# An expert gather of 8 tokens x 16 picks of one head, with the weighted sum in four column positions

## The reference, cut to what matters

```python
def peer_ffn(h, w_query, keys1, keys2, expert_u, expert_v):
    q = (hf @ w_query).reshape(t, PEER_HEADS, 2, PEER_HALF)
    s1 = einsum('thc,hnc->thn', q[:, :, 0], keys1)        # 128 keys a side
    s2 = einsum('thc,hnc->thn', q[:, :, 1], keys2)
    v1, i1 = top_k(s1, 16); v2, i2 = top_k(s2, 16)
    cand_s = v1[..., :, None] + v2[..., None, :]          # 256 candidates
    cand_i = i1[..., :, None] * 128 + i2[..., None, :]
    top_s, top_pos = top_k(cand_s, 16)
    idx = take_along_axis(cand_i, top_pos); gate = softmax(top_s)
    # for every token, 8 heads x 16 picks:
    act = gelu(einsum('thkd,td->thk', expert_u[idx], h))
    out = einsum('thk,thkd->td', gate * act, expert_v[idx])
```

## Time and profile before

| | us |
|---|---|
| median of 3 runs | 3149.2 |
| lowest, highest | 3148.14, 3149.35 |
| span of the profiled execution | 3147.3 |
| begin of the stage `peer` in it | 1745.2 |
| first gather issued | 1761.0 |
| last product of gathered rows begins | 3133.3 |

### The profile page before, as it was taken

One profiled execution on the slowest core, in us unless ns is written; L12 is line 12 of the kernel. 1 busy time (PEld: TensorE's weight loads), 2 busy tenths in 40 slices (PEclk: granted clock), 3 DMA queues, 4 the chain that ended last, 5 costly groups with the idle time before them and its releaser, 6 DMA issues. The chain is left out here.

```text
span 3147.3 us, 27781 instructions
## 1 busy us (share of the span) xinstructions
PE 2714.7 (86%) x10052; PEld 1434.7 (46%) x10052; DVE 1357.1 (43%) x3261; ACT 590.2 (19%) x1357; POOL 708.3 (23%) x622
## 2 busy tenths in 40 slices
PE   8999697877888888769989899999988888888887
PEld 5755343333333333244768666666543343333332
DVE  2162300000000000044531676667777777777774
ACT  2132100000000000022120222322322322222222
POOL 0000000000000000001420233334434444444442
PEclk9899799999888999979999999999999999999989
DMA  4002699999999999531224799999999999999997
GB/s 146 27 21 113 263 426 426 427 426 426 426 424 423 420 418 421 251 137 47 94 67 149 290 426 425 425 418 421 400 426 427 412 426 426 427 414 426 420 421 329
DMA packets 138856, 1049.63 MB, mean 334 GB/s; under 512 B 22032, under 2 KB 23008, under 8 KB 48224
## 3 DMA queue, kind: packets, MB, share of 16 engines
q0 software_dynamic: 82944, 545.32, 41.5%
q1 hardware_dynamic: 55776, 502.53, 38.8%
HBM read 1051.96 MB, written 20.97 MB: 341 GB/s over the span
## 5 line engine op out<-in xcount | busy, mean ns | idle before, releaser
L2184 PE MATMUL psum<-peer_ring,peer_diag 128*128 128x512 f32 x2048 | 956.8, 619 | 154.2 <-ACT peer_diag L2245 154.1
L2037 POOL DMA_INDIRECT peer_ring<-in_peer_uv,peer_pick x512 | 576.5, 1126 | 910.7 <-PE psum L2184 746.6
L2353 DVE CUSTOM_DVE_ANT_0 peer_ring<-peer_ring,sb_rows 128x1024 f32<-128x1024 f32 x512 | 625.1, 1225 | 348.6 <-DMA peer_ring<-in_peer_uv,peer_pick 337.2
L2184 PEld LDWEIGHTS psum<-peer_ring,peer_diag 128*128 128x128 f32 x2048 | 396.6, 198 | 666.3 <-issue 430.7
L1120 PE MATMUL psum<-ffn1w_w,sb_y 128*64 128x512 f32 x1872 | 510.4, 649 | 85.9 <-DMA ffn1w_w<-in_w_up 60.0
L1165 DVE TENSOR_TENSOR sb_y<-psum,sb_y 128x512 f32<-128x512 f32 x32 | 22.1, 692 | 877.0 <-ACT sb_y L1148 877.0
L1120 PEld LDWEIGHTS psum<-ffn1w_w,sb_y 128*64 128x64 f32 x1872 | 176.1, 149 | 346.7 <-issue 345.0
L2245 ACT ACTIVATE peer_diag<-sb_ident,peer_mix 128x128 f32<-128x128 f32 x512 | 178.1, 395 | 683.7 <-DVE peer_mix L2363 681.9
L1141 PE MATMUL psum<-ffn1w_w,moe_hT 128*64 128x512 f32 x864 | 227.8, 598 | 36.0 <-DVE moe_hT L1170 33.7
L1213 POOL DMA_INDIRECT expert_rows<-sb_tiles,ffn_block_tok x32 | 32.3, 1009 | 894.6 <-ACT sb_tiles L1154 894.6
L1516 PE MATMUL psum<-sb_y,sb_tiles 128*128 128x256 f32 (+1 forms) x640 | 189.5, 455 | 17.3 <-ACT mix_Q L1741 8.9
(11 more groups left out here) (429 smaller groups left out, 2498.0 us busy)
## 6 DMA issues: line engine op xcount, KB each, us to landing
ffn1w_w<-in_w_gate SPq DMA_DIRECT2D x64, 2048.0 KB, 31.6
ffn1w_w<-in_w_down SPq DMA_DIRECT2D x54, 2048.0 KB, 35.8
ffn1w_w<-in_w_up SPq DMA_DIRECT2D x53, 2048.0 KB, 34.3
sb_tiles<-in_w_in2b SPq DMA_DIRECT2D x56, 512.0 KB
sb_rows<-in_w_up SPq DMA_DIRECT2D x11, 2048.0 KB, 36.0
sb_rows<-in_w_down SPq DMA_DIRECT2D x10, 2048.0 KB, 32.2
sb_tiles<-in_w_query SPq DMA_DIRECT2D x30, 512.0 KB
sb_tiles<-in_w_out SPq DMA_DIRECT2D x24, 512.0 KB
```

The source lines that it names most:

```text
L2037: pool.indirect_dma_start(out=ring[:, slot], out_offset=None, in_=A["peer_uv"], in_offset=bass.IndirectOffsetOnAxis(ap=pick[:, i, j:j + 1] ...
L2184: last = nc.tensor.matmul(ps[:, BANK[i] + c], diag[:, b % DIAGS, x], ring[:, slot, D + 512 * c:D + 512 * (c + 1)], start=False, stop=end, ...
L2353: dve.tensor_tensor_reduce(ring[:, n % RING, 0:D], ring[:, n % RING, 0:D], hr[:, i], 1.0, 0.0, ALU.mult, ALU.add, dots[:, i, j + x:j + x + ...
```

## The change

Everything but `peer` and its tables stays. What a gather holds, and what follows from it, is changed:

- A gather holds all 16 picks of one head for 8 tokens (row 16a + c is pick c of token a). Four of them, for tokens 8q.. of each 32-token strip, make a batch: (tile, head, quarter q). There are 128 batches of four gathers in place of 256 of two, the ring has 8 slots in place of 10, and a slot is released with its whole batch (`spent` once a batch). The gathers are 512 of 1 MiB as before.
- The weighted sum of a gather takes a 128x32 block, of which 8 columns are nonzero, in place of a 128x128 diagonal: VectorE writes `mix` (128 x 4 x 8) from the turned gates and the gelu, ScalarE's diagonals are gone, and TensorE runs the batch's four gathers into four strips of 32 PSUM partitions: 8 products of 512 columns a batch (`weighted_sum`).
- The dot product needs, in each partition, the row of its own token: `spread` makes it on TensorE (two products with a contraction over 32 rows for each half of 512 columns) and `spread_out` copies it with ScalarE (128x1024, twice a pair) into `hb`, three pairs deep. A pair serves two gathers for as many heads as a set has; the sets are `SETS`: heads 1, 1, 2, 4 in tile 0, 8 in tile 1, 4, 4 in tile 2, 8 in tile 3. That makes 64 pairs, 32 of them in tile 0.
- The picks and gates of a group are turned: VectorE spreads them over 128 columns (`placed`), TensorE multiplies and transposes (`turn`), VectorE and ScalarE copy them out.
- Groups go tile by tile, head by head. The searches keep three pieces and VectorE as their place, but not their even pace: 6 in steps 0 to 28, 8 in steps 30 to 61 (one per 4 steps, a step being two gathers), 8 in steps 102 to 133, 8 in steps 144 to 183 (one per 5).
- Ahead of the first gather TensorE and ScalarE now do three spread pairs, `residual(0)`, `scores(1)` and `turn(0)`. Three more small constants are loaded.
- In the second step of a batch TensorE's weighted sum comes ahead of that step's other products, not behind. The late products stand two steps apart from step 2 to 88; the gates are not stored but go from PSUM through a sigmoid over both halves.

```diff
-RING = 10
+RING = 8
...
+BATCH, QUARTERS = 4, 4
+SETS = ((1, 1, 2, 4), (8,), (4, 4), (8,))
+BATCHES, PER = NT * P * PEER_H * TOPK // P // BATCH, TOPK // BATCH
...
+def _batches():
+    for i, sizes in enumerate(SETS):
+        head = 0
+        for size in sizes:
+            for quarter in range(QUARTERS):
+                QUADS.append((i, quarter, size, len(BATCH_OF)))
+                BATCH_OF.extend((i, hd, quarter) for hd in range(head, head + size))
+            head += size
...
+def last_reader(pair):
+    quad, side = divmod(pair, 2)
+    return BATCH * (QUADS[quad][3] + QUADS[quad][2] - 1) + 2 * side + 1
+
+SPREADS_AT = {}
+for _quad in range(2, len(QUADS)):
+    _start, _wide = QUADS[_quad][3], QUADS[_quad - 1][2] > 1
+    SPREADS_AT.setdefault(_start - (2 if _wide else 1), []).append(2 * _quad)
+    SPREADS_AT.setdefault(_start - 1, []).append(2 * _quad + 1)
+SPREADS_AT.setdefault(0, []).insert(0, 3)
...
+SEARCH = {2: (0, 1, 2), 3: (5, 6, 8), 4: (10, 12, 13), 5: (15, 17, 18), 6: (20, 22, 23), 7: (25, 27, 28)}
+for _g in range(8, 16):
+    _s = 30 + 4 * (_g - 8)
+    SEARCH[_g] = (_s, _s + 1, _s + 3)
+for _g in range(16, 24):
+    _s = 102 + 4 * (_g - 16)
+    SEARCH[_g] = (_s, _s + 1, _s + 3)
+for _g in range(24, 32):
+    _s = 144 + 5 * (_g - 24)
+    SEARCH[_g] = (_s, _s + 2, _s + 4)
...
-    for g in range(10):
-        JOBS_AT.setdefault(8 * g, []).append(("query", 6 + g))
-        if g % 2:
-            JOBS_AT.setdefault(8 * g + 4, []).append(("scores", 3 + g // 2))
-    for j in range(3 * KH + LATE):
-        JOBS_AT.setdefault(4 + 7 * j // 4, []).append(("conv", j) if j < 3 * KH else ("late", j - 3 * KH))
-    JOBS_AT.setdefault(82, []).append(("late_sum", 0))
+    for r, at in zip(range(3, 8), ((0, 1, 3), (5, 6, 8), (10, 11, 13), (15, 16, 18), (20, 21, 23))):
+        for b, job in zip(at, (("query", 2 * r), ("query", 2 * r + 1), ("scores", r))):
+            JOBS_AT.setdefault(b, []).append(job)
+    late = [("conv", j) for j in range(3 * KH)]
+    for m in range(KD):
+        late += [("gate_a", m), ("gate_b", m), ("branch", m)]
+    late += [("result", m) for m in range(KD)]
+    for j, job in enumerate(late):
+        JOBS_AT.setdefault(2 + 2 * j, []).append(job)
+    JOBS_AT.setdefault(2 * len(late) + 5, []).append(("late_sum", 0))
...
+        at = 98 + 4 * h
+        for b, job in ((at, ("query", QUERIES + 2 * h)), (at + 1, ("query", QUERIES + 2 * h + 1)), (at + 3, ("scores", PEER_H + h))):
+            JOBS_AT.setdefault(b, []).append(job)
+    for b, job in ((100, ("rows", 2)), (112, ("rows", 3))):
...
+        near = st.sb("near", [P, 3, 2, P])
+        far = st.sb("far", [P, H, 2, P])
+        work = st.sb("work", [P, 3, HT])
...
+        hb = st.sb("hb", [P, HB, D])
...
-                for n in range(NT * PICKS):
-                    g, slot = n // K, n % RING
-                    i, j = tile_of(g), head_of(g) * K + n % K
-                    if n % K == 0:
+                pool.memset(mix[:], 0.0).then_inc(cleared, 1)
+                for n in range(BATCH * BATCHES):
+                    b, slot = n // BATCH, n % RING
+                    i, hd, quarter = BATCH_OF[b]
+                    g = H * i + hd
+                    if n == BATCH * FIRST_BATCH[g]:
                         pool.wait_ge(picked, g + 1)
                     if n >= RING:
-                        pool.wait_ge(spent, n - RING + 1)
+                        pool.wait_ge(spent, (n - RING) // BATCH + 1)
+                    at = quarter + QUARTERS * (n % BATCH)
                     pool.indirect_dma_start(out=ring[:, slot], out_offset=None, in_=A["peer_uv"],
-                                            in_offset=bass.IndirectOffsetOnAxis(ap=pick[:, i, j:j + 1], axis=0)
+                                            in_offset=bass.IndirectOffsetOnAxis(ap=pick[:, g, at:at + 1], axis=0)
...
+                def spread(pair):
+                    quad, side = divmod(pair, 2)
+                    i, quarter = QUADS[quad][0], QUADS[quad][1]
+                    bank = spread_bank(pair)
+                    pe.wait_ge(r_out, 2 * i + 2)
+                    if pair == 0:
+                        pe.wait_ge(loaded, 80)
+                    if bank == 0:
+                        pe.wait_ge(done, 1)
+                    if bank == 2 and pair > 2 * QUAD_OF[FIRST_BATCH[2 * H]]:
+                        pe.wait_ge(done, 2)
+                    if bank == 0 and pair > 2 * QUAD_OF[FIRST_BATCH[3 * H]]:
+                        pe.wait_ge(done, 3)
+                    for c in range(2):
+                        if pair or c:
+                            pe.wait_ge(hb_out, 2 * pair + c)
+                        for x in range(2):
+                            r = slice(SPAN * (2 * side + x), SPAN * (2 * side + x + 1))
+                            last = nc.tensor.matmul(ps[:, bank + x], copies[r, P * quarter:P * (quarter + 1)],
+                                                    hr[r, i, 512 * c:512 * (c + 1)], start=True, stop=True)
+                        last.then_inc(hb_ps, 1)
+                def turn(g):
+                    pe.wait_ge(placed_in, g + 1)
+                    if g == 0:
+                        pe.wait_ge(loaded, 80)
+                    else:
+                        pe.wait_ge(gates_out, g)
+                    nc.tensor.matmul(ps[:, 5, P:P + K], placed[:, 0], eights[:], start=True, stop=True)
+                    nc.tensor.transpose(ps[:, 5, 0:P], placed[:, 1], ident[:]).then_inc(turned, 1)
...
+                def weighted_sum(b):
+                    i, _, quarter = BATCH_OF[b]
+                    pe.wait_ge(mixed, b + 1)
+                    for c in range(2):
+                        for r in range(BATCH):
+                            slot = (BATCH * b + r) % RING
+                            last = nc.tensor.matmul(ps[SPAN * r:SPAN * (r + 1), sums_bank(i) + c],
+                                                    mix[:, b % DIAGS, r, EDGE - 8 * quarter:EDGE - 8 * quarter + SPAN],
+                                                    ring[:, slot, D + 512 * c:D + 512 * (c + 1)],
+                                                    start=False, stop=b == LAST_BATCH[H * i + H - 1], skip_group_check=True)
+                    last.then_inc(spent, 1)
...
                 scores(0)
                 pe.wait_ge(scaled, 1)
-                rows(0, 0)
-                rows(1, 2)
+                rows(0, 2)
+                pe.wait_ge(s_out, 1)
                 query(2)
                 query(3)
-                pe.wait_ge(r_out, 4)
+                pe.wait_ge(r_out, 2)
+                for pair in range(3):
+                    spread(pair)
                 residual(0)
-                residual(1)
                 scores(1)
+                turn(0)
+                rows(1, 6)
                 query(4)
                 query(5)
                 scores(2)
-                for b in range(BATCHES):
-                    i, j = place(b)
-                    for name, m in JOBS_AT.get(b, ()):
+                turn(1)
+                for step in range(STEPS):
+                    b = step // 2
+                    if step % 2 == 0:
+                        for pair in SPREADS_AT.get(b, ()):
+                            spread(pair)
+                    if step % 2 == 1:
+                        if b in (FIRST_BATCH[H], FIRST_BATCH[2 * H], FIRST_BATCH[3 * H]):
+                            residual(BATCH_OF[b][0])
+                        weighted_sum(b)
...
-                            result(m - OUT)
-                    pe.wait_ge(diagonal, BATCH * (b + 1))
-                    for x in range(BATCH):
-                        slot = (b * BATCH + x) % RING
-                        end = j + x == PICKS - 1
-                        for c in range(2):
-                            last = nc.tensor.matmul(ps[:, BANK[i] + c], diag[:, b % DIAGS, x], ring[:, slot, D + 512 * c:D + 512 * (c + 1)],
-                                                    start=False, stop=end, skip_group_check=True)
-                        last.then_inc(spent, 1)
...
+                    if step - 1 in PICKS_AT:
+                        turn(PICKS_AT[step - 1])
...
+                def spread_out(pair):
+                    bank = spread_bank(pair)
+                    for c in range(2):
+                        act.wait_ge(hb_ps, 2 * pair + c + 1)
+                        if c == 0 and pair >= HB // 2:
+                            act.wait_ge(dotted, last_reader(pair - HB // 2) + 1)
+                        act.activation(hb[:, hb_of(pair):hb_of(pair) + 2, 512 * c:512 * (c + 1)], ps[:, bank:bank + 2],
+                                       ACT.Copy).then_inc(hb_out, 1)
...
-                def diagonals(b):
-                    act.wait_ge(mixed, b + 1)
-                    if b >= DIAGS:
-                        act.wait_ge(spent, BATCH * (b - DIAGS + 1))
-                    for x in range(BATCH):
```

(53 more changed lines are left out.)

338 lines of the change are left out of this document (181 added, 157 removed).

## The result

| | before | after |
|---|---|---|
| median of 4 runs, us | 3149.27 | 3525.04 |
| lowest, highest | 3148.14, 3149.85 | 3519.64, 3532.31 |
| span of the profiled execution | 3147.3 | 3517.8 |

A forecast was written before the change was run, and what follows sets the result against it. The prediction took the kernel before to be bound by DMA bytes. Its terms, mostly late gathers, less 15 for gaps and 2 for the tail, summed to +110 us, giving 3259 us, range 3165 to 3380.

The forecast's parts named there:

- the stream's gaps: Gaps in the DMA stream of gathers would come back: -15 us (-22 to 0).
- the sum: TensorE's weighted sum of a batch, four column positions at once: 1.7 us, 3.5 at half clock.
- rival B: Column positions go only two at a time, sum 3.4 us: 3340 to 3580 us, chance 0.13.
- Rivals A and C: A: stream stays full, 3149 to 3200 us, chance 0.22. C: faster through evenly freed slots, 3139 us, chance 0.05.
- the start: First gather issued at 1775 in place of 1760.96, behind three spread pairs and other work: +14 us (12 to 20).
- 1.55 from issue to bytes: In the ring's loop, a gather's first bytes come 1.55 us behind its issue on GpSimd.
- the loop of the ring: From a batch's last landing to the first byte two batches on: 8.1 us, 9.9 at half clock.
- the quiet loop fits, barely: Without search pieces, 8.1 to 9.9 us a turn against 9.82 of DMA cover: +4 us (0 to 40), some 55 batches.
- terms 4, 5 and 7: Batches 8 to 15 +8 us, batches 16 to 31 +16, steps 144 to 183 +20, with search pieces lengthening the loop.
- term 6: Steps 102 to 133, VectorE 22.1 us against 22.1, loop with a slower TensorE: +20 us (0 to 40).
- batches 0 to 7: First ring +3 us (0 to 6); then TensorE's queue of spreads, 136 us against 96 of DMA: +36 (15 to 60).

The follow-up runs named there:

- experiment 13: The changed kernel with `scores(1)` and `turn(0)` ahead of the first three spread pairs, ScalarE's order likewise: 3555.16 us, ratio 1.1284.
- experiment 8: The kernel before with eight ring slots in place of ten, given back four at a time: 3564.65 us, ratio 1.132.
- Experiment 1: The changed kernel with VectorE mixing a batch right behind its own fourth product, not behind the next batch's first: 3371.36 us, ratio 1.0703.
- experiment 10: The changed kernel with ten slots for eight, spreads behind the first pair left out for room: 3243.94 us, against 3450.69 with eight slots and spreads left out.

## Why the prediction was wrong, point by point

**Right: what bounds before, the sign, and who loses.** Before is bound by bytes, and the loss is gathers that start too late. The forecast's list of places is the list that the trace shows, and each term but the stream's gaps (-15) has its sign.

**Right: the sum.** Four column positions run side by side: 16 recorded matmuls in 1.93 us at full clock (3240.01 above) and 3.65 at half, for a forecast of 1.7 and 3.5. That excludes rival B, though its span of times, 3340 to 3580, holds the result; pairs would show 3.4 at full clock. Rivals A and C needed a full stream, which the stretch's 325 GB/s excludes. The Trainium skill (TensorE: Matmul & The Clock Gate, Packing small matmuls) had led to an estimate of 2.2 us at full clock; the trace's 1.93 is between that and the forecast's.

**Right: the start.** The first gather is issued at 1776.42 for a forecast of 1775, and a half pair takes 2.26 us for 2.2 (1867.43 to 1869.69 below). Start +16 for +14, though the stage's begin alone varies by 8 us between executions (experiment 13).

**Wrong, and the costliest: "1.55 from issue to bytes" (the loop of the ring).** The step took a slice's edge for the first byte: by the packet records the first row starts at 1762.73, 1.77 us behind the issue, and not at 1762.5. And it took the bytes to come at 426 GB/s from that moment. The row itself gave 180 GB/s for that half microsecond, and I passed over it. By experiment 8 the full rate comes 1.5 us later, with 0.43 MB missing by then, 1.0 us of the full stream. From issue to landing, 1.55 + 2.46 = 4.0 us in the forecast, measured 6.12: 2.1 more, and the loop's 9.9 us at half clock become 12.0, as measured. The ramp explains 1.0 of the 2.1; the rest is there when the gather ahead has not landed yet (the table above), and no run explains it. Part of it is that the engines run apart: the 16 records of one gather are spread over 1.4 us in after's late batches, so some engines have nothing to do before the gather has landed. The Trainium skill (DMA: Bandwidth & Descriptors, Anatomy of one DMA) fits such a transfer with 2.0 us and its bytes at 436 GB/s, an estimate of 4.4 us here; measured are 5.0 at the shortest and 6.12 in after, and the measurement decides.

**Wrong with it: "the quiet loop fits, barely", so that 56 batches cost 4 us.** They cost 89. A loop longer than its cover isn't hidden a little, it is paid in full in every turn: 12.02 less 9.94 in each of batches 97 to 126. The forecast saw 9.9 against 9.82 and gave the term a mean of 0.07 us a batch; with the loop uncertain by 2 us on one side, the term should have been 0 to 2 us each, 0 to 110, not 0 to 40.

**Wrong in size, in the main by the same step: terms 4, 5 and 7.** They were costed as a piece's length less 1.2 us of slack. There was no slack but a deficit of 2, which every piece adds to: +106 for +44. Experiment 1 gets 154 us back by taking the next gather out of the loop, and experiment 10 shows 207 from two slots, 70 of them in batches 16 to 32 and 72 to 91.

**Wrong by a wait that it didn't have: term 6, +82 for +20.** In steps 102 to 133 VectorE stands 34 us waiting for scores that TensorE does only behind the weighted sum, and ten slots bring back only 12 of the 82 us. The forecast wrote that the sum ahead of its step's products saves 3.6 us on the ring's loop; it didn't ask which products were now late.

**Wrong in size: batches 0 to 7, +73 for +3 and +36.** One of their turns, TensorE's and its partners' queue (timeline):

```profile
1865.58 1.93 PE L2255 MATMUL psum<-peer_ring,peer_mix 128*32 128x512 f32 x16
...
1867.43 1.13 PE L2185 MATMUL psum<-sb_rows,peer_copies 32*128 32x512 f32 x4
...
1868.61 1.02 ACT L2361 ACTIVATE peer_hb<-psum 128x1024 f32<-128x1024 f32 x1 [5.78 <-PE psum L2185]
...
1869.69 1.73 PE L2185 MATMUL psum<-sb_rows,peer_copies 32*128 32x512 f32 x4 [1.12 <-ACT peer_hb L2361]
...
1872.63 2.08 PE L2185 MATMUL psum<-sb_rows,peer_copies 32*128 32x512 f32 x4 [1.21 <-ACT peer_hb L2361]
...
1875.82 2.08 PE L2185 MATMUL psum<-sb_rows,peer_copies 32*128 32x512 f32 x4 [1.11 <-ACT peer_hb L2361]
...
1879.09 0.19 DVE L2511 TENSOR_TENSOR peer_mix<-peer_gates,peer_acts 128x32 f32<-128x32 f32 x1 [2.01 <-ACT peer_acts L2378]
...
1879.69 3.93 PE L2207 MATMUL psum<-sb_y,sb_tiles 128*128 128x256 f32 x16
...
1883.55 1.93 PE L2255 MATMUL psum<-peer_ring,peer_mix 128*32 128x512 f32 x16
...
1885.78 0.94 POOL L2110 DMA_INDIRECT peer_ring<-in_peer_uv,peer_pick  x1 [12.93 <-PE psum L2255]
```

Four halves take 10.5 us here. With gaps of 1.1 to 1.2 us between them the granted clock fell, and a half's matmuls took 2.08 for 1.13: a half of 3.2 us, not 2.2. The mean over the stretch is 0.79 where the forecast took full clock. TensorE fills the stretch of 160 us: it is busy 125.5 us and waits 23.0 for ScalarE's copies. By its groups, with the idle time ahead of them, spreads take 72, products 61, sums 19 and the rest 9, for a forecast of 136 in all. And the forecast set that against the 96 us that the moved bytes would need, and counted seven intervals of eight, where before took 87 for all eight. 160 less 87 is the 73.

**Wrong: "gaps that come back" (-15).** They only come back in a full stream. A gain that rests on one case of the loop shouldn't have stood in a sum beside terms of the other.

**What the forecast said would show it.** Issue near 1775: yes. Below 300 GB/s in the 140 us behind it: yes, 272 from 1776 to 1916. TensorE's gaps ended by the copies into `hb`: yes, 23.0 of the 34.5 us from 1788 to 1948. GpSimd's waits in fours: yes. Clock 0.5 late: yes. 420 or more between steps 62 and 100: no, 393 and 385 in the slices that hold those steps. That view alone would have told that the quiet loop didn't fit.

**What stays open.** Why a gather's first rows take longer than 0.309 us; why its pitch depends on its lead up to 6 us, when an empty queue lands one in 5.0 to 5.5; what the clock's return alone would win; what scores a step or two earlier would win; and the 30 us of experiment 13. More slots with the spreads in place weren't tried, since they don't fit beside `hb`. No version ran faster than before.

## What to carry to other kernels

A ring is measured by its lead: how long before the landing ahead of it a gather can be issued, in the worst place of the loop, against the time that a gather needs on an empty queue. Read that time from issue to landing where the queue was empty, never from issue to first byte. Slots that are given back in groups take the group's time off the lead, and one instruction that is queued behind the next landing (here the mixing) takes a landing off it; when a loop's length and its cover come out within a microsecond or two, give the case in which it doesn't fit its full price, the difference times the number of turns. And when one product is moved ahead of others in an engine's order, look at who waits for those others.

## What the runs showed of the hardware that I had not expected

- A 1.049 MB gather on an empty queue: first row 1.8 us behind the issue, the first 16 rows of 8 KB 0.92 us each on average where later ones take 0.309, 418 GB/s from 3 us behind the issue on, landed 5.0 us behind the issue at the shortest. In a full stream a gather lands every 2.47 us.
- With a gather still under way, the next one's landing went, in these kernels, with how early it was issued: pitch 3.86 us at a lead of 2.26, 3.01 at 4.32, 2.47 at 6.42.
- Four 128x32 float32 column positions run side by side: 8 products of 512 columns in 1.93 us at full clock, 3.65 at half.
- In the turn shown, gaps of 1.1 to 1.2 us between groups of matmuls of 1.13 us were followed by half the clock: the same four took 2.08.
- The 16 engines of a gather need not end together: with a stream that never ran dry (before) one record came 3.3 us behind the other 15, at the same pitch of 2.5 us.
